# Attention inside a decoder layer: score tiles turned over by 64-key products with the identity instead of 128-key transposes

## What is computed

```python
s_c = jnp.einsum('bgrqd,bgcd->bgrqc', qblk, kc) * ATTN_SCALE - slopes * dist_c
p_c = masked_softmax(s_c, dist_c >= 0)
o_c = jnp.einsum('bgrqc,bgcd->bgrqd', p_c, vc)
...
p_s = masked_softmax(s_s, mask_s)
o_s = jnp.einsum('bgrqm,bgqmd->bgrqd', p_s, vs)
...
p_w = masked_softmax(s_w, mask_w)
o_w = jnp.einsum('bgrqk,bgkd->bgrqd', p_w, vw)
return gblk[..., 0:1] * o_c + gblk[..., 1:2] * o_s + gblk[..., 2:3] * o_w
```

## Time and profile before

| | us |
|---|---|
| median of 3 runs | 2393.32 |
| lowest and highest | 2392.87, 2393.83 |
| the profiled execution | 2393.82 |
| its span in the trace | 2392.2 |
| attention's units, first scores to last values | 370.2 to 640.3 |

### The profile page before, as it was taken

The page is one execution under the profiler, slowest core; times in us unless marked ns, Lnnn a source line. Parts: engine busy times, 40 slices in busy tenths (PEclk is TensorE's granted clock), DMA queues, the critical chain, the costliest instruction groups (busy, mean ns, idle before and its releaser), DMA issues. The chain is left out here.

```text
span 2392.2 us, 84238 instructions
## 1 busy us (share of the span) xinstructions
PE 2272.3 (95%) x33744; PEld 1559.7 (65%) x33744; DVE 957.4 (40%) x3183; ACT 335.9 (14%) x917; POOL 857.8 (36%) x1672
## 2 busy tenths in 40 slices
PE   6999999999999699999999999999999999999994
PEld 3878876555544367767777777776776667776563
DVE  2222226776356433333333333333333333333333
ACT  0000006776411100000000000000000000000001
POOL 1100004544214543434343434344443434444333
PEclk8999999999999799999999999999999999999997
DMA  9423042000234687476769494968869988989994
GB/s 314 163 90 109 1 121 71 2 1 2 77 119 145 222 313 278 143 270 210 272 212 340 147 341 145 342 207 297 313 229 384 349 285 303 380 292 390 391 370 160
DMA packets 195573, 526.26 MB, mean 220 GB/s; under 512 B 45416, under 2 KB 75264, under 8 KB 195328
## 3 DMA queue, kind: packets, MB, share of 16 engines
q1 hardware_dynamic: 142496, 479.22, 53.4%
q0 software_dynamic: 33808, 40.21, 8.2%
q10 hardware_dynamic: 19088, 4.47, 0.9%
HBM read 489.98 MB, written 33.35 MB: 219 GB/s over the span
## 5 line engine op out<-in xcount | busy, mean ns | idle before, releaser
L1670 PE MATMUL psum<-w_ring,xT 128*32 128x256 f32 x18304 | 1038.5, 380 | 28.5 <-issue 25.6
L1670 PEld LDWEIGHTS psum<-w_ring,xT 128*32 128x32 f32 x18304 | 693.7, 110 | 322.0 <-issue 48.6
L1682 PE MATMUL psum<-w_ring,actT 128*32 128x256 f32 x9152 | 528.7, 380 | 9.3 <-DMA w_ring<-in_w_down 7.7
L1682 PEld LDWEIGHTS psum<-w_ring,actT 128*32 128x32 f32 x9152 | 329.5, 110 | 166.0 <-DVE actT L1735 36.5
L1599 POOL TENSOR_TENSOR scalars<-scalars 128x1 f32<-128x1 f32 x578 | 109.9, 190 | 749.5 <-DVE xT L1739 657.4
L1717 ACT ACTIVATE sig<-glu 128x128 f32<-128x128 f32 x286 | 88.6, 310 | 1471.4 <-DVE glu L1726 1471.4
L1618 POOL DMA_INDIRECT x_rows<-y_out,scalars_i x145 | 233.9, 1613 | 43.7 <-issue 43.4
L1724 DVE TENSOR_TENSOR psum<-psum,up_bias 128x256 f32<-128x256 f32 x143 | 61.8, 432 | 410.3 <-PE psum L1670 400.1
L1748 DVE SCALAR_TENSOR_TENSOR y_out<-psum,scalars,gate_q 128x256 f32<-128x256 f32 x143 | 69.2, 484 | 300.0 <-PE psum L1682 220.9
L719 POOL TENSOR_SCALAR scores<-scores,coef 128x64 f32<-128x64 f32 (+5 forms) x128 | 133.5, 1058 | 147.7 <-DVE coef L926 147.7
L1608 POOL DMA_INDIRECT x_gathered<-h_rows,scalars_i x144 | 153.5, 1066 | 79.4 <-issue 77.4
(11 more groups left out here) (241 smaller groups left out, 2009.6 us busy)
## 6 DMA issues: line engine op xcount, KB each, us to landing
w_ring<-in_w_gate_up SPq DMA_DIRECT2D x256, 1024.0 KB, 16.0
w_ring<-in_w_down SPq DMA_DIRECT2D x128, 1024.0 KB, 19.9
ada_then_cmp_in<-in_w_ada SPq DMA_DIRECT2D x16, 1024.0 KB, 7.0
ada<-in_w_ada SPq DMA_DIRECT2D x8, 1024.0 KB, 6.9
xt<-in_x SPq DMA_DIRECT2D x8, 512.0 KB, 9.8
w_uv_then_w_out<-in_w_in SPq DMA_DIRECT2D x4, 1024.0 KB, 11.7
x_rows_in<-in_x SPq DMA_DIRECT2D x8, 512.0 KB, 4.2
x_rows<-x SPq DMA_DIRECT2D x8, 512.0 KB, 2.9
```

The costliest lines, as they stand in the source:

```text
L1670: last = nc.tensor.matmul(psU[h][j * BLK:(j + 1) * BLK, :], xT[:, k, :], w[:, j], start=(h == 0 and k == 0), stop=(k == KD - 1))
L1682: last = nc.tensor.matmul(psO[m * BLK:(m + 1) * BLK, :], actT[h][:, k, :], w[:, m * Q:(m + 1) * Q], start=False, stop=(h == 1 and k == KD ...
```

## The change

Three edits, all in `attend`:

- `transpose_rows` no longer uses the transpose. For each tile and `g` it issues two products with the identity: keys 0 to 63 of the tile stationary, result on partitions 0 to 63 of `psT`, and keys 64 to 127, result on partitions 64 to 127. The compressed slice gives one such product.
- `vc` has 128 rows, with rows from 63 on zero, and `weigh_values` contracts over all 128 rows for the compressed group. Rows 64 to 127 of `pT` hold there what an earlier group left; they meet zeros.
- POOL zeroes the four `pT` buffers once, after `vc`, and DVE's wait on `s_zero` goes from 2 to 6.

```diff
-    vc = sb("v_cmp", [NCP, P])
+    vc = sb("v_cmp", [P, P])
...
+        for i in range(4):
+            nc.gpsimd.memset(pT[i][:], 0.0).then_inc(s_zero, 1)
...
             for t, (b, kt, c0) in enumerate(tiles):
-                m = NCP if b == B_CMP else P
                 for g in range(2):
-                    last = nc.tensor.transpose(psT[at % 2][0:m, (2 * t + g) * P:(2 * t + g + 1) * P],
-                                               score[n % (LAG + 1)][g][:, c0:c0 + m], ident[:])
+                    c = slice((2 * t + g) * P, (2 * t + g + 1) * P)
+                    for h in range(1 if b == B_CMP else 2):
+                        last = nc.tensor.matmul(psT[at % 2][half(h), c],
+                                                score[n % (LAG + 1)][g][:, c0 + h * HALF:c0 + (h + 1) * HALF], ident[:],
+                                                start=True, stop=True)
...
-                        v, p = vc[:, g * HD:(g + 1) * HD], pT[at % 4][0:NCP, c]
+                        v, p = vc[:, g * HD:(g + 1) * HD], pT[at % 4][:, c]
...
-        dve.wait_ge(s_zero, 2)
+        dve.wait_ge(s_zero, 6)
```

## The result

| | before | after |
|---|---|---|
| median of the runs | 2393.10 (2390.64 to 2393.83, 4 runs) | 2418.54 (2418.17 to 2426.14, 4 runs) |
| the profiled execution | 2393.82 | 2426.14 |
| its span | 2392.2 | 2424.5 |
| attention, from the start of the first scores to the start of the last value record | 269.8 | 301.8 |

The ratio is 1.012 with a 95% interval of 1.0104 to 1.0136, so 25 to 33 us slower by the medians.

A forecast was written before the change was run, and what follows sets the result against it. The prediction took PE to bound the attention. Doubled records (+57.7), compressed groups (+7.0) and fewer changes of form (-33.7) sum to +31.0 us on the profiled 2393.82, giving 2424.8 us, range 2416 to 2440.

The forecast's parts named there:

- PE bounds the attention: In the attention PE is busy 256.53 of 257.00 us, so each nanosecond added to its queue adds to the time.
- allowed for the start: First 10 us of the attention's units, PE at 0.50 of its clock: 1 or 2 us either way.
- Twice the records at 0.109 us for two, +57.7: Turning over 528 full tiles: four records instead of one, halves side by side in 2 x 0.109 us, +57.7 us.
- not side by side: Rival: the halves do not overlap since both read the same identity; a further +115 us, 2540; chance 0.02.
- Compressed groups, +7.0: Turning over compressed tiles: two products share partitions 0 to 63 and cannot overlap, 64 x 0.109 = +7.0 us.
- The row it leaned on: L750, eight records into one partition range, 0.40 us, against L746 over two halves, 0.28 us: one half costs double.
- Fewer changes of form, -33.7: PE's queue: at 232 places where transposes and values meet, the 0.148 or 0.12 us change of use goes, -33.7 us.
- The rival 2458.5: Rival: the changes of use between transposes and values do not vanish, the 33.7 us stay, 2458.5; chance 0.04.
- Open loads of the halves: Rival: 1184 load steps of the halves on PE stand open at 0.05 us, +59 us, 2484; chance 0.03.
- Memsets, cost 0: POOL's four 128x512 memsets, 2.4 us in all, are covered by the compression: cost 0; uncovered 1 to 5 us.
- The range had 5 us for this: Later stages entered 31 us later can meet another clock phase: 5 us for one half-clock stretch more or less.

The follow-up runs named there:

- e5: Changed kernel without the second halves (keys 64 to 127 of every tile not turned over, copies take 64 rows): 2429.11 us, attention 301.0 us.
- e3: Changed kernel, but each 128x128 tile turned over by one product with the identity, 128 stationary columns, not by two halves: 2451.97 us, attention 336.9 us.
- e6: Changed kernel, but compressed groups turned over into both partition halves, g = 0 into 0 to 63, g = 1 into 64 to 127: 2412.36 us, attention 296.0 us.
- e2: Changed kernel, but compressed values weighed over 64 rows as before: 2426.61 us, attention 308.5 us.
- e4: Kernel before, with its transposes, but PE weighs values two groups at a time instead of after each: 2382.04 us, attention 265.3 us.
- e8: Kernel before, values weighed in pairs of groups only from the third query block on: 2380.76 us, attention 257.6 us.
- e1: Changed kernel run once more as it was, on another occasion, for a second trace: 2419.92 us, attention 301.8 us.
- e10: Kernel before, values in pairs of groups from the third query block on, compressed values padded to 128 rows: 2374.01 us, attention 254.0 us.
- e11: As e10, but three groups of values behind three of transposes: 2373.64 us, attention 255.5 us.
- e12: As e10, but scores computed two pieces at a time from the third query block on: 2369.68 us, attention 254.4 us.

## Why the prediction was right

The forecast was 2424.8, the range 2416 to 2440. Measured were 2418.54, near the lower end of the range, and 2426.14 for the profiled execution, to which the sum was tied. The attention is where the sum is tested, and it agrees closely; that the profiled execution came within 1.3 us of the forecast is partly luck, since it was the longest of four.

- **PE bounds the attention.** Held: it absorbed nothing that the traces show; attention +32.0 us for a sum of +31.0. Of the 32.0, 1.7 us is a stretch of half clock of 13.7 us instead of 10.2, about what had been allowed for the start.
- **Twice the records at 0.109 us for two, +57.7.** Held: 0.87 us for a group of halves; e5 shows that the second halves cost under 1 us in all, e3 that whole products take the same time apart from the changes of form. The rival "not side by side" (2540) fell.
- **Compressed groups, +7.0.** Held: 5.8 us came back in e6. The row it leaned on did not show it: 0.28 against 0.40 us in the earlier trace rows is no doubling. And the 0.37 us for four value records over 128 rows does not stand in the earlier trace rows, which has only those over 64 rows; the trace of the kernel before has it (0.369 us, four places).
- **Fewer changes of form, -33.7.** Held, and by the mechanism named: e3 puts the changes back and costs 35.0 us more, e2 puts 47 of them back and costs 6.7, and e4 and e8 take them from the kernel before, with no other instruction. The prediction saw two groups back to back at only one place, 12 records in 0.80 us; behind that place stand compressed values over 64 rows, so its 0.15 us was already one between values and values. Group by group in the trace before, the price is the same elsewhere: eight value records take 0.588 us at each of 47 places ahead of transposes. What the sum had not separated is what makes a form: between products it is the rows and columns in use (e2, e3, e8), while transposes form one kind whatever their columns (e8). The rival 2458.5 fell.
- **Open loads of the halves** did not come: 8 steps take 0.87 us. So the statement of the Trainium skill ("TensorE: Matmul & The Clock Gate", Part 3) that a load overlaps running matmuls only where the row group differs does not hold here. All halves use the same 128 rows, their loads are hidden, and the measurement decides. The page "TensorEngine Tiling (Array Packing)" of the Trainium skill (Key Properties) says that changing the tiling mode, not just the tile, drains TensorE. With that the traces agree, at 0.15 us for each change of form.
- **Memsets, cost 0.** Held: the four took 1.93 us for the 2.4 estimated and ended 19 us ahead of their reader (POOL's and DVE's timelines):

```profile
349.15 1.93 POOL L713 MEMSET probT<- 128x512 f32 x4
```

```profile
370.66 0.23 DVE L895 COPY k_cmpT<-psum 128x63 f32<-128x63 f32 x1 [1.06 <-PE psum L752]
```

What was off: the +31 us was meant for the profiled execution, whose difference is 32.3, but the medians differ by 25.4, and by 27.4 on the second occasion. The other three executions of the changed kernel had a mean granted clock of 0.979 to 0.981 against 0.978, and e1's trace puts such a difference into the experts' stage; for those three themselves no trace shows where it lies. The range had 5 us for this, and used them.

## What to carry to other kernels

Before trading a costly form of work for one that matches its neighbours, price both from the starts in the timeline: the work itself (here +64.7 us for 592 tiles) and the changes of form (here 232 at 0.15 us). When the changes are the prize, look first whether the order alone can take them away. Here pairs of groups with the original transposes, and the padding, gained 17 us where the changed form lost 25 to 33.

## What the runs showed that I had not expected

- The stretch of half clock at the start of the attention was 10.2 us long in the kernel before, 13.7 in the changed one, and 27.2 in e4, whose PE was busy 26.44 us of it. Leaving the first two blocks in their old order brought 10.2 back (e8, e10, e11), though e12 had 17.1. With one trace for each kernel this is a hint, not a cause shown.
